# The order of eight experts, their sums by one-hot products and some waits, in a two-layer decoder trunk

## The reference

```python
for l in range(2):
    h = rms_norm(x, mix_norm[l])
    p = h @ w_comb                       # 3200 columns (and 16 more in layer 1)
    y = concat[rwkv7_mix(...), short_conv_mix(...), dilated_attention_mix(...)]
    x = x + y @ w_o[l]
    h = rms_norm(x, ffn_norm[l])
    if l == 0:
        x = x + swiglu(h, dense_wg, dense_wu, dense_wd)     # 1024 -> 3584 -> 1024
    else:
        x = x + moe_swiglu(h, router, moe_wg, moe_wu, moe_wd)
# moe_swiglu: each token goes to its top 2 of 8 experts; each expert is a SwiGLU of
# the same shape, and its rows are weighted by a softmax gate and added to the token
```

## Time and profile before

| | |
|---|---|
| median of 3 runs | 1436.35 us (1435.61 to 1437.4) |
| the profiled execution | 1437.15 us, its span 1435.3 us |
| TensorE busy | 1413.2 us (98%) |
| VectorE, ScalarE busy | 874.6 us (61%), 722.7 us (50%) |
| read from HBM | 434.96 MB, 305 GB/s over the span |
| mean granted clock of TensorE | 0.998 |

### The profile page before, as it was taken

One profiled execution on the slowest core, in us unless ns is written; L12 is line 12 of the kernel. 1 busy time (PEld: TensorE's weight loads), 2 busy tenths in 40 slices (PEclk: granted clock), 3 DMA queues, 4 the chain that ended last, 5 costly groups with the idle time before them and its releaser, 6 DMA issues.

```text
span 1435.3 us, 24792 instructions
## 1 busy us (share of the span) xinstructions
PE 1413.2 (98%) x10420; PEld 1088.3 (76%) x10420; DVE 874.6 (61%) x1149; ACT 722.7 (50%) x991; POOL 72.2 (5%) x61
## 2 busy tenths in 40 slices
PE   8999999999999999999999999999999999999997
PEld 7988999999999889734888534888435888888532
DVE  6586865555577887311999212999103999899300
ACT  6545544444455645201888202888104887888200
POOL 0005000001000050000000000000000000000000
PEclk9999999999999999999999999999999999999999
DMA  9610455555535410999999999999999999999996
GB/s 344 213 46 4 164 218 177 186 191 181 177 120 221 140 61 3 401 422 420 421 421 421 421 421 421 421 421 420 422 421 421 420 415 422 408 420 418 345 423 273
DMA packets 64838, 440.83 MB, mean 307 GB/s; under 512 B 8001, under 2 KB 10577, under 8 KB 12113
## 3 DMA queue, kind: packets, MB, share of 16 engines
q1 hardware_dynamic: 63344, 434.46, 75.0%
q0 software_dynamic: 960, 3.15, 1.4%
q10 hardware_dynamic: 416, 1.57, 0.3%
HBM read 434.96 MB, written 2.62 MB: 305 GB/s over the span
## 4 chain that ended last, share of the span: by engine, by line
PE 89%; DMA 5%; DVE 3%; ACT 1%; issue 1%; SPq 0%; POOL 0%; DVEq 0%; ACTq 0%; POOLq 0%
PE bank L896 19%; PE bank L898 19%; PE bank L897 19%; PE bank L877 12%; PE bank L1631 11%; PE bank L1649 5%; DMA arena<-in_moe_wu 5%; PE bank L1594 1%; PE bank L1639 1%; DVE w_lo L2299 1%; DMA ring<-in_w_in 1%; PE bank L1664 1%; PE bank L1069 0%; DVE w_lo L2607 0%; ACT w_hi L1774 0%
## 5 line engine op out<-in xcount | busy, mean ns | idle before, releaser
L1774 ACT ACTIVATE w_hi<-ring 128x1024 fp32r<-128x1024 f32 x284 | 298.6, 1060 | 173.2 <-PE bank L898 167.0
L896 PE MATMUL bank<-w_hi,acts_hi 128*128 128x512 f32 x672 | 265.1, 394 | 0.0
L898 PE MATMUL bank<-w_hi,acts_lo 128*128 128x512 f32 x672 | 261.8, 390 | 0.0
L897 PE MATMUL bank<-w_lo,acts_hi 128*128 128x512 f32 x672 | 261.7, 389 | 0.0
L896 PE MATMUL bank<-acts_hi,w_hi 128*128 128x256 f32 x796 | 227.2, 285 | 1.6 <-DVE acts_lo L2545 0.8
L897 PE MATMUL bank<-acts_lo,w_hi 128*128 128x256 f32 x796 | 225.2, 283 | 0.0
L898 PE MATMUL bank<-acts_hi,w_lo 128*128 128x256 f32 x796 | 225.1, 283 | 0.0
L2616 DVE TENSOR_TENSOR w_lo<-arena,w_hi 128x1024 fp32r<-128x1024 f32 x144 | 175.2, 1224 | 13.0 <-ACT w_hi L1774 7.2
L2616 DVE TENSOR_TENSOR w_lo<-ring,w_hi 128x1024 fp32r<-128x1024 f32 x144 | 174.5, 1223 | 13.2 <-ACT w_hi L1774 7.7
L1774 ACT ACTIVATE w_hi<-arena 128x1024 fp32r<-128x1024 f32 x144 | 152.8, 1064 | 37.1 <-PE bank L898 37.1
L2977 DVE TENSOR_TENSOR arena<-arena,bank 128x256 f32<-128x256 f32 x28 | 11.8, 422 | 260.0 <-ACT arena L2207 260.0
(11 more groups left out here) (323 smaller groups left out, 1921.2 us busy)
## 6 DMA issues: line engine op xcount, KB each, us to landing
ring<-in_moe_wu SPq DMA_DIRECT2D x56, 1024.0 KB, 23.5
ring<-in_moe_wg SPq DMA_DIRECT2D x56, 1024.0 KB, 22.5
arena<-in_moe_wd SPq DMA_DIRECT2D x56, 1024.0 KB, 23.2
arena<-in_moe_wu SPq DMA_DIRECT2D x52, 1024.0 KB, 22.0
arena<-in_moe_wg SPq DMA_DIRECT2D x36, 1024.0 KB, 21.0
ring<-in_moe_wd SPq DMA_DIRECT2D x32, 1024.0 KB, 20.4
ring<-in_w_in SPq DMA_DIRECT2D x24, 1024.0 KB, 6.2
late<-in_moe_wg SPq DMA_DIRECT2D x16, 1024.0 KB, 22.8
```

Source lines behind the costliest of these rows:

```text
L896: pe.matmul(out_, a_hi, b_hi, start=first, stop=False, **kw)
L897: pe.matmul(out_, a_hi, b_lo, start=False, stop=False, **kw)
L898: return pe.matmul(out_, a_lo, b_hi, start=False, stop=final, **kw)
L1774: return act.activation(o, i, ACT.Copy, **kw)
```

## The change

- The order of the seats is B A A B A B A B. The full pair now stands in seats 1 and 2, so `behind_full` holds for seat 2.
- `LAST_SUM` is 5: the outputs of the first five seats are summed by one-hot products (at seats 3 and 5), and those of the last three are added in HBM.
- TensorE's wait for `yg_kept` moves from behind `begin` into the next expert, behind the column products of chunk 1.
- In the expert of `behind_full`, ScalarE's `begin` (the copy into `xb`) moves ahead of the last down split.
- The first two k of the first chunk of each layer: all high times high products first, waiting only for `hi_ready` and `u_high`, then those with `w_lo`, then those with the low part of x.

```diff
-SEATS = tuple({"A": P, "B": C}[kind] for kind in "BABABAAB")
+SEATS = tuple({"A": P, "B": C}[kind] for kind in "BAABABAB")
...
-LAST_SUM = 4
+LAST_SUM = 5
...
                 for q in range(PIECES):
-                    pe.wait_ge(lo_ready, IN0[l, ch] + q + 1)
+                    if ch == CHUNKS[0] and q == 0:
+                        pe.wait_ge(hi_ready, IN0[l, ch] + 1)
+                    else:
+                        pe.wait_ge(lo_ready, IN0[l, ch] + q + 1)
...
+                            for kk in range(2):
+                                pe.wait_ge(u_high, KT * l + kk + 1)
+                                first_pair(w_hi, hi, (kk,), True)
+                            pe.wait_ge(lo_ready, IN0[l, ch] + 1)
+                            first_pair(w_lo, hi)
+                            pe.wait_ge(u_low, KT * l + 2)
+                            last = first_pair(w_hi, lo)
+                            continue
+                        if ch == CHUNKS[0] and k == 1:
                             continue
...
-            def full_chunks(seen, before_last=None):
+            def full_chunks(seen, before_last=None, outs=0):
...
                     column_chunk("u", j, seen)
+                    if outs and j == 1:
+                        pe.wait_ge(yg_kept, outs)
...
                     half_columns(j, 1, seen)
+                    if q and j == 1:
+                        pe.wait_ge(yg_kept, seen.outs)
...
                     begin(q + 1)
                     down(NJ - 1, seen)
-                    pe.wait_ge(yg_kept, after.outs)
...
                 if q + 1 < NE:
                     begin(q + 1)
-                    pe.wait_ge(yg_kept, after.outs)
...
+                if early:
+                    early()
                 split("d", NJ - 1, seen, range(0, TURN_AT))
                 turned(NJ - 1, seen)
                 split("d", NJ - 1, seen, range(TURN_AT, 4))
...
-                    full_chunks(seen, {3: write_rows} if q == LAST_SUM + 1 else {})
+                    full_chunks(seen, {3: write_rows} if q == LAST_SUM + 1 else {},
+                                (lambda: begin(q + 1)) if behind_full(q) else None)
...
-                if q + 1 < NE:
+                if q + 1 < NE and not behind_full(q):
                     begin(q + 1)
```

More of the change, by code:

```diff
@@ L1010, in project_together, with first_pair @@
                         if ch == CHUNKS[0] and k == 0:
[L1011 to L1019, removed]
+                            def first_pair(a, x, order=(0, 1), opens=False):
+                                for kk in order:
+                                    for m, (kind, n) in enumerate(mine):
+                                        b, at, _ = bank_place(l, us0 + m)
+                                        ws = slice(kk * CW + n % 4 * P, kk * CW + (n % 4 + 1) * P)
+                                        ins = pe.matmul(bank[b][:, at:at + T], a[:, q, ws], x[:, kk, :],
+                                                        start=opens and kk == 0 and m % 2 == 0, stop=False,
+                                                        skip_group_check=True)
+                                return ins
+                            for kk in range(2):
[7 more added lines that the diff above has]
+                        if ch == CHUNKS[0] and k == 1:
                             continue
@@ L1686, in expert @@
             def expert(q):
-                seen, after = seen_before(q), seen_before(q + 1)
+                seen = seen_before(q)
                 if behind_full(q):
-                    full_chunks(seen, lambda: gather_half(q + 3, hot[(q + 1) % 2]))
+                    full_chunks(seen, lambda: gather_half(q + 3, hot[(q + 1) % 2]), seen.outs)
                     pe.wait_ge(gate_ready, q - 1)
@@ L1694, in expert @@
                     down(NJ - 1, seen)
-                    pe.wait_ge(yg_kept, after.outs)
                     return
                 if SEATS[q] == P:
-                    full_chunks(seen)
+                    full_chunks(seen, outs=seen.outs)
                 else:
@@ L2171, in turned, with full_chunks @@
                 copy(at_hi[:, j % 2, :], bank[6][:, :]).then_inc(at_kept, 1)
-            def full_chunks(seen, hooks={}):
+            def full_chunks(seen, hooks={}, early=None):
                 for j in range(1, NJ):
```

## The result

The kernel after takes **1443.39 us** (median of 5 runs, 1443.09 to 1443.91); the kernel before, run beside it on the same chip, takes 1437.32 us (1435.61 to 1437.54). The ratio is **1.0049, 95% interval 1.0038 to 1.0059**: 6 to 7 us slower. The forecast was 1443.5, range 1437.0 to 1447.0. The profiled execution took 1443.91 us, its span is 1442.0 us (before: 1437.15 and 1435.3).

A forecast was written before the change was run, and what follows sets the result against it. TensorE and the load stream were taken to bound the kernel together. Stream losses of +8.4 us less 1.3 for the start gave +7.1 on the median 1436.35: 1443.5 us, range 1437.0 to 1447.0.

The forecast's parts named there:

- What bounds: In the last 860 us TensorE and the load stream are both full; a later stream end costs its whole delay.
- Start: At the first product, TensorE waits for w_hi, not w_lo: 0.9 or 1.7 us gained, 1.3 taken.
- the upper case: At the program's start, TensorE's earlier start keeps its clock at 2.4 GHz: 1.7 us gained.
- ScalarE's copy, kept output: Among the experts, TensorE's two waits for ScalarE go away: -1.3 and -1.4 us.
- Sums: The fourth expert's two sums have three terms, the new full one 1.9 us each time: +3.8 us.
- TensorE alone: TensorE's own work over start, removed waits, longer sums and short waits for loads: -0.8 us.
- The holes: Transfer lost at changes from full to half experts: 10.3, then 4.8, then nothing; 6.7 us before.
- the floor: Shortest time of a load from issue to landing, 5.0 us; further gaps in issues mean idle DMA engines.
- The stream's end: The load stream ends 7.1 us later: losses +8.4, earlier start -1.3.
- The last expert: There TensorE, which would have ended 0.8 us earlier, waits about 8 us.
- Rival 4: Waiting in the last expert, TensorE drops to 1.2 GHz; three such chunks add 20 us, 1463; chance 0.04.
- Rivals 1 to 3: Stream doesn't bind, 1435.5 (0.10); only second handover's loss goes, 1438.7 (0.08); stream losses stay, sums shorter, 1432.4 us (0.02).

The follow-up runs named there:

- e2: Kernel before with one in three loads of the last six experts cut to half its bytes (their numbers wrong): 1435.46 us, 0.9989 of before.
- e11: Kernel before with only ScalarE's copy and the wait for the kept output moved; order, sums and start as before: 1435.33 us, 0.9989 of before.
- e3: Kernel before with the new expert order and the sums for the first five alone; start, ScalarE's copy and kept output unchanged: 1446.95 us, 1.0067 of before.
- e1: Kernel after with one in three loads of the last six experts cut to half its bytes (their numbers wrong): 1435.35 us, 0.9988 of before.
- e4: Kernel after with the experts in the order B A B A A B A B, the full pair in the middle: 1440.79 us, 1.0024 of before.
- e6: Kernel after in the order B A B A B A B A, without a full pair, sums for the first four: 1448.09 us, 1.0082 of before.
- e7: Kernel after with the one-hot sums for the first three experts alone, the later five scattered: 1443.36 us, 1.0049 of before.
- e9: Kernel after with one in three loads of its third expert alone cut to half its bytes (numbers wrong): 1443.82 us, 1.0048 of before.
- e8: Kernel after with one in three loads of its last expert alone cut to half its bytes (numbers wrong): 1435.46 us, 0.9992 of before.
- e5: Kernel after with the order and sums of before, so only start, ScalarE's copy and kept output are moved: 1433.74 us, 0.9980 of before.

## Why the prediction was right

By its own steps:

- **What bounds.** "TensorE and the load stream arrive together" holds as far as the runs can tell: e2 takes the loads away from before and gains 1.9 us (0.1 to 3.0), e11 takes 2.7 us of waits away and gains 1.8.
- **Start.** The clock did not fall, the upper case (1.7). The further w_lo started DVE's chain of three where it did, and the next piece's product came at 15.01 where 14.95 was worked out. In the traces DVE's first w_lo to the first expert product takes 587.5, 587.8 and 587.6 us without the edit (before, e2, e3) and 586.3, 586.0 and 586.4 with it (after, e1, e4): that is 1.4 us. With all thirteen traces it is 1.6: 587.6 on average in the four kernels without the edit (e11 has 587.7) and 586.05 in the nine with it (585.9 to 586.4). 1.3 was taken, between the two cases, and the case that came is the upper one. In each kernel with the moved product order the clock was full from 11 us on. From the Trainium skill ("TensorE: Matmul & The Clock Gate", Part 1: The HAM clock gate), by which the throttled state is the default and activity releases it, I had drawn that the lower level would stay; here it didn't come, and the trace decides.
- **ScalarE's copy, kept output.** Both waits are gone, -2.7 on TensorE as said.
- **Sums.** The two of the fourth expert take 1.06 + 3.64 = 4.70 us each, 1.72 more for the new term each time and not 1.9: +3.4 for +3.8. A full term alone behind the half one takes 1.9 us; two take 3.64. A small miss.
- **TensorE alone.** In the experts -2.7 + 3.8 = +1.1 was forecast without the short waits, and +0.7 with the 3.4 that the sums measured; e1 against e2 shows +1.2, 0.3 of it a wait for a load. With the start nothing is left, and the two kernels without the load limit are level.
- **The holes.** Behind the pair 10.3 forecast, 11.3 measured; at the next handover 4.8 and 4.8; at the last none, and none is there. Before 6.7 and 6.5. So the losses grew by 9.6 and not by 8.4. The count is rougher than these values look: the load issued first behind the last handover takes 11.5 us and not 7.7, as e6's takes 17.5 and not 13.6, both nearly 4 us more. In after nothing hung on it, since both values are above the floor; in e6 it was a good part of the miss. Which term is too small stays open. The estimate of 4.5 us for the floor, from the Trainium skill ("DMA: Bandwidth & Descriptors", Anatomy of one DMA), rests on a fit that the page makes for transfers issued by GpSimd; these are SyncE's, and the traces have 4.9 and 5.1.
- **The stream's end.** 7.1 later forecast, 1425.2 to 1431.7 = 6.5 measured. Here errors cancel, and that the number came out so close (1443.39 against 1443.5) is in part luck. The losses are 1.2 larger, but 0.52 MB less is written (2.10 against 2.62). I had said that the scatter which goes is one of half an expert, 0.25 MB; the bytes are those of a full one, and at 421 GB/s that is 1.2 us. The start gave 0.3 more than counted. A last 0.3 is within the reading of slices.
- **The last expert.** "TensorE waits about 8 us": 4.9 us of waits, and 1.7 us of work that the lower clock stretched to 3.4, together 6.6.
- **Rival 4** happened in its condition and not in its price. The clock fell behind a wait of 1.99 us, but for 3.41 us once and not for three chunks, and in that time TensorE had a wait for loads ahead of it in any case. e3, e7 and e9 have the same fall in the last expert, e4 and e8 have none ahead of their last product, and each follows the stream's count. That a slower clock only fills a wait that TensorE has anyway fits these runs; none of them changes the clock alone.
- **Rivals 1 to 3** fell: the rate dropped to 350, the second handover lost 4.8, and the sums are 4.7 each.

What stays open: the gain of e11 falls 0.9 short of the waits removed, and its interval (0.3 to 2.9) doesn't exclude either value; and the 4 us by which the first load behind the last handover was counted too short.

## What to carry to other kernels

Two resources that are both nearly full exchange slack through the buffers between them; follow the slack (here the time from issue to landing) from stage to stage and cut it at both ends, at the floor where the source stands still and at the ceiling where the consumer waits. Time lost at the floor leaves no mark on the consumer until a later stage (here the last; in e7 in part the sixth), so look for it in the transfer rate and not in the waits. What an edit on the consumer is worth depends on which end it moves the slack toward: here moving one pair of stages, with the sums that go with it, cost 9.6 us (e3 over before), and the start and the waits taken away beside it gave back 3 (e5 under before).

## What the runs showed of the hardware

Where TensorE had work and its clock fell to half (1.2 GHz), it stood there for 3.41 us: at the start of before (12.16 to 15.58), of e2, e3 and e11, in the last expert of after (1402.67 to 1406.08), of e3, e7 and e9, and in e6 (1281.3 to 1284.7). Each time it came behind 2 to 3 us without products (2.99, 1.99 and 3.10 in the three with times), but the length of the wait alone doesn't tell: waits of 2.20 us in after, 2.73 in e4, 2.84 in e6 and 2.82 in e7 passed without a fall. The start of the whole program shifts by about 1 us from one execution to the next: DVE's first w_lo comes at 11.00, 11.03, 10.12, 9.89, 10.59 and 9.91 us in before, after, e1, e2, e3 and e4. Differences of under a microsecond between two single traces therefore have to be read from a common mark on, and not from the span.
